# The spatial gating's layernorm, moved behind its transposes

## The reference

```
def _spatial_gating(u, v, ln_g, ln_b, w_s, b_s):
    u = jax.nn.gelu(u)
    v = _layernorm(jax.nn.gelu(v), ln_g, ln_b)          # mean and variance over the 256 channels
    vr = v.reshape(bn, ln // 128, 128, 4, ch // 4)
    mixed = jnp.einsum("gpq,bnqgc->bnpgc", w_s, vr) + b_s.T[None, None, :, :, None]
    return u * mixed.reshape(bn, ln, ch)
```

## Time and profile before

| what | value |
|---|---|
| median of three runs | 2793.08 us |
| the profiled execution's own time | 2795.46 us |
| its span, first to last instruction | 2793.7 us |
| TensorE busy | 2563.4 us, 92% of the span |
| VectorE busy | 1490.1 us, 53% |
| ScalarE busy | 727.0 us, 26% |
| GpSimd busy | 1051.5 us, 38% |

### The profile page before, as it was taken

How to read it: one execution, slowest core, us unless ns; L and a number is a source line. 1 busy time by engine, 2 the same in 40 slices (tenths; PEclk the granted TensorE clock), 3 DMA queues, 4 the chain that set the end, 5 groups by cost and what they waited for, 6 DMA issues and landing times.

```text
span 2793.7 us, 33113 instructions
## 1 busy us (share of the span) xinstructions
PE 2563.4 (92%) x12016; PEld 2054.9 (74%) x12016; DVE 1490.1 (53%) x2191; ACT 727.0 (26%) x1208; POOL 1051.5 (38%) x493
## 2 busy tenths in 40 slices
PE   8889999999989779999895999979889999999997
PEld 4768787777768767777674778868667777777775
DVE  5793036574711256544888544466764444444446
ACT  4311243434300045212312354433221000011012
POOL 2233333333346433447651111113554444333344
PEclk9999999999999889999997799989999999999998
DMA  7674453434366753233311222251211111111111
GB/s 281 227 290 173 131 159 128 142 124 136 125 222 204 292 205 143 74 129 125 130 46 51 63 80 77 67 182 42 68 61 46 46 46 45 47 51 45 45 45 68
DMA packets 131232, 325.24 MB, mean 116 GB/s; under 512 B 11568, under 2 KB 59248, under 8 KB 125616
## 3 DMA queue, kind: packets, MB, share of 16 engines
q1 hardware_dynamic: 93392, 223.50, 24.1%
q10 hardware_dynamic: 37728, 100.22, 9.9%
HBM read 248.57 MB, written 70.39 MB: 114 GB/s over the span
## 4 chain that ended last, share of the span: by engine, by line
PE 49%; DVE 8%; issue 3%; ACT 1%; DMA 0%; DVEq 0%; POOL 0%; SPq 0%; ACTq 0%
PE pb L478 36%; PE g L2981 6%; PE g L3054 2%; PE pb L2981 1%; PE g L3034 1%; DVE zcs L2246 1%; PE g L2962 1%; DVE f_spare L2455 1%; PE g L2835 1%; DVE xl L2158 0%; DMA kept_in<-cs_d 0%; PE g L2960 0%; DVE hl L2525 0%; DVE ml L2462 0%; DVE cb L2504 0%
## 5 line engine op out<-in xcount | busy, mean ns | idle before, releaser
L845 POOL TENSOR_TENSOR w_hi<-w_raw,one 128x1024 fp32r<-128x1024 f32 x191 | 399.7, 2093 | 1543.1 <-PE pb L478 1136.1
L478 PE MATMUL pb<-xh,w_hi 128*128 128x512 f32 (+1 forms) x1224 | 485.9, 397 | 46.2 <-POOL w_lo L848 17.0
L848 POOL TENSOR_TENSOR w_lo<-w_raw,w_hi 128x1024 fp32r<-128x1024 f32 x191 | 510.1, 2671 | 15.0
L478 PE MATMUL pb<-xh,w_lo 128*128 128x512 f32 (+1 forms) x1224 | 477.1, 390 | 0.0
L478 PE MATMUL pb<-xl,w_hi 128*128 128x512 f32 (+1 forms) x1224 | 476.5, 389 | 0.0
L478 PEld LDWEIGHTS pb<-xh,w_hi 128*128 128x128 f32 x1224 | 235.7, 193 | 103.2 <-POOL w_lo L866 16.3
L478 PE MATMUL pb<-mh,w_hi 128*128 128x512 f32 x704 | 283.5, 403 | 15.0 <-DVE ml L2462 7.3
L478 PE MATMUL pb<-mh,w_lo 128*128 128x512 f32 x704 | 281.4, 400 | 0.0
L478 PE MATMUL pb<-ml,w_hi 128*128 128x512 f32 x704 | 281.2, 399 | 0.0
L478 PEld LDWEIGHTS pb<-xl,w_hi 128*128 128x128 f32 x1224 | 234.8, 192 | 51.6
L478 PEld LDWEIGHTS pb<-xh,w_lo 128*128 128x128 f32 x1224 | 235.4, 192 | 50.2 <-issue 1.0
(11 more groups left out here) (408 smaller groups left out, 4614.0 us busy)
## 6 DMA issues: line engine op xcount, KB each, us to landing
w_raw<-in_wall SPq DMA_DIRECT2D x205, 512.0 KB, 3.5
mod_later<-in_modw SPq DMA_DIRECT2D x28, 1024.0 KB, 6.1
proj_d<-stage ACTq DMA_DIRECT2D x40, 512.0 KB, 2.7
at_bias<-in_bias SPq DMA_DIRECT2D x64, 192.0 KB, 2.7
mod_raw<-in_modt SPq DMA_DIRECT2D x8, 1024.0 KB, 10.7
svt<-vt_d ACTq DMA_DIRECT2D x12, 512.0 KB, 4.6
vc<-proj_d SPq DMA_DIRECT2D x10, 512.0 KB, 5.7
vt_d<-spare_h ACTq DMA_DIRECT2D x10, 512.0 KB, 3.8
```

The costliest lines, as they stand in the source:

```text
L478: mm = pe.matmul(pb[bank][:, 0:n], w[:, b, wc:wc + P], x[:, k, tokens], start=(count == 0), stop=(count == total - 1))
L845: nc.gpsimd.tensor_tensor(w_hi[:, b, :], w_raw[:, b, :], one[:, 0:1].to_broadcast([P, 1024]), ALU.mult).then_inc(w_high, 1)
L848: nc.gpsimd.tensor_tensor(w_lo[:, b, :], w_raw[:, b, :], w_hi[:, b, :], ALU.subtract).then_inc(w_split, 1)
```

## The change

The values are no longer normalised while channels lie on the partitions. The sixteen transposes come first, straight from `zcs[:, 6:8]`. With tokens on the partitions, mean and variance are sums along a row, one number per partition and chunk, kept in the new small tile `vstat`: ScalarE takes them with the accumulator output of eight copies (sum) and eight squares with the negative mean as bias (sum of squares), takes the square root of eight numbers per partition, VectorE inverts them, and ScalarE normalises in eight instructions. Both `gating_means` go. The channel scale and bias no longer act on `v`: the scale comes into the eviction of the gating products (line 2299 before), and the bias, times the row sums of `w_s`, is added to `sgb_sb` once, from four small matmuls into the fifth bank of `g`. SyncE's bias loads wait for ScalarE's squares in place of VectorE's multiplication.

```diff
--- before.py
+++ after.py
@@ -144,6 +144,7 @@
         both_gain = keep("both_gain", [P, KT])
         both_root = keep("both_root", [P, KT])
         dec = keep("dec", [P, NC, 8])
+        vstat = keep("vstat", [P, 4, NCX])
         ident, mean_d, mean_v, mean_g = (mat[:, n, :] for n in range(4))
         arena = place["next"]
 
@@ -368,8 +369,7 @@
         low_keys, z_at = at("zkr", [P, TA], arena + 107 * KB, F32R)
         zcs, a = at("zcs", [P, 8, T], z_at)
         hpad, a = at("hpad", [P, 2, T + TAPS - 1], a)
-        vsq, b = at("vsq", [P, 2, T], a)
-        vroot, _ = at("vroot", [P, T], a)
+        vsq, b = at("vsq", [P, NCX, C], a)
         vtok, c_ = at("vtok", [P, NCX, 256], b)
         sgw_sb, c_ = at("sgw_sb", [P, 4, P], c_)
         sgb_sb, _ = at("sgb_sb", [P, 2, P], c_)
@@ -787,8 +787,7 @@
                 bc, br, j = step_of(s)
                 sp.dma_start(at_bias[:, s % 4, :], bias6[br, bc, s // 16, j]).then_inc(bias_in[s % 4], 16)
 
-            sp.wait_ge(y_pe, 2)
-            sp.wait_ge(y_dve, 3)
+            sp.wait_ge(y_act, 2)
             for s in range(4):
                 bias_load(s)
             for s in range(STEPS):
@@ -1450,27 +1449,32 @@
                 return pb[u % 2]
 
             u_k, u_v, u_q, u_k1, _ = PAIR_UNITS
+            act.wait_ge(y_pe, 2)
+            for n in range(NCX):
+                v = act.activation(vtok[:, n, :], g[:, n // 2, C * (n % 2):C * (n % 2) + C], ACT.Copy,
+                                   accum_out=vstat[:, 0, n:n + 1])
+            v.then_inc(y_act, 1)
             pair_k_high(0, 0, pair_unit(u_k))
             act.wait_ge(y_dve, 1)
-            act.activation(vsq[:, :, :], zcs[:, 6:8, :], ACT.Square).then_inc(y_act, 1)
+            act.wait_ge(xl_ready, 6 * KT)
+            for n in range(NCX):
+                v = act.activation(vsq[:, n, :], vtok[:, n, :], ACT.Square, bias=vstat[:, 0, n:n + 1],
+                                   accum_out=vstat[:, 1, n:n + 1])
+            v.then_inc(y_act, 1)
+            act.wait_ge(y_act, 2)
+            act.activation(vstat[:, 1, :], vstat[:, 1, :], ACT.Sqrt, scale=1.0 / C,
+                           bias=epsc[:, 0:1]).then_inc(y_act, 1)
             for n in (1, 2):
                 pair_k_high(0, n, pair_unit(u_k + n))
-            act.wait_ge(y_pe, 2)
-            act.activation(vroot[:, :].rearrange("p (u n) -> p u n", u=2), g[:, 4:6, :], ACT.Sqrt,
-                           bias=epsc[:, 0:1]).then_inc(y_act, 1)
             pair_values(0, 0, pair_unit(u_v), bank_free[u_v % 2])
             keys_across(0)
             pair_values(0, 1, pair_unit(u_v + 1), bank_free[(u_v + 1) % 2])
             act.wait_ge(y_dve, 3)
-            for t in range(2):
-                n, m = COL["sg_g"] + t, COL["sg_b"] + t
-                v = act.activation(zcs[:, 6 + t, :], zcs[:, 6 + t, :], ACT.Identity,
-                                   scale=col[:, n:n + 1], bias=col[:, m:m + 1])
+            for n in range(NCX):
+                v = act.activation(vtok[:, n, :], vtok[:, n, :], ACT.Identity, scale=vstat[:, 1, n:n + 1],
+                                   bias=vstat[:, 2, n:n + 1])
             v.then_inc(y_act, 1)
             pair_values(0, 2, pair_unit(u_v + 2), bank_free[u_v % 2])
-            act.wait_ge(y_pe, 3)
-            act.activation(vtok[:, :, :].rearrange("p (a n) c -> p a (n c)", a=4), g[:, 0:4, :],
-                           ACT.Copy).then_inc(y_act, 1)
             for n in range(2):
                 pair_q_high(0, n, pair_unit(u_q + n))
             queries_across(0)
@@ -1478,7 +1482,7 @@
             act.activation(zcs[:, 2:4, :], zcs[:, 0:2, :], ACT.Square).then_inc(z_act, 1)
             for n in range(2):
                 if n == 0:
-                    act.wait_ge(y_pe, 4)
+                    act.wait_ge(y_pe, 3)
                 pair_k_high(1, n, pair_unit(u_k1 + n))
             act.wait_ge(y_dve, 5)
             act.dma_start(cs_d[0:2].rearrange("t p n -> p t n"), zcs[:, 6:8, :]).then_inc(kept_out, 16)
@@ -2253,21 +2257,21 @@
             for k in range(KT):
                 ctx_low(k)
             taps(5, 14)
+            nc.vector.tensor_scalar(vstat[:, 3, 0:2], col[:, COL["sg_b"]:COL["sg_b"] + 2], float(C), None, ALU.mult)
+            dve.wait_ge(y_act, 1)
+            nc.vector.tensor_scalar(vstat[:, 0, :], vstat[:, 0, :], -1.0 / C, None, ALU.mult).then_inc(y_dve, 1)
+            dve.wait_ge(y_dve, 1)
             dve.wait_ge(y_pe, 1)
             for t in range(2):
-                v = nc.vector.tensor_tensor(zcs[:, 6 + t, :].rearrange("p (u n) -> p u n", u=2),
-                                            zcs[:, 6 + t, :].rearrange("p (u n) -> p u n", u=2),
-                                            g[:, 4:6, :], ALU.subtract)
-            v.then_inc(y_dve, 1)
+                nc.vector.scalar_tensor_tensor(sgb_sb[:, t, :], g[:, 4, P * t:P * t + P], vstat[:, 3, t:t + 1],
+                                               sgb_sb[:, t, :], ALU.mult, ALU.add)
             for n, (first, last) in enumerate(((14, 17), (17, 18), (18, 20))):
                 pair_k_low(0, n, pb[(u_k + n) % 2], bank_free[(u_k + n) % 2])
                 taps(first, last)
-            dve.wait_ge(y_act, 2)
-            nc.vector.reciprocal(vroot[:, :], vroot[:, :]).then_inc(y_dve, 1)
+            dve.wait_ge(y_act, 3)
+            nc.vector.reciprocal(vstat[:, 1, :], vstat[:, 1, :]).then_inc(y_dve, 1)
             dve.wait_ge(y_dve, 2)
-            nc.vector.tensor_tensor(zcs[:, 6:8, :], zcs[:, 6:8, :],
-                                    vroot[:, :].unsqueeze(1).to_broadcast([P, 2, T]), ALU.mult)\
-              .then_inc(y_dve, 1)
+            nc.vector.tensor_tensor(vstat[:, 2, :], vstat[:, 0, :], vstat[:, 1, :], ALU.mult).then_inc(y_dve, 1)
             for n, (first, last) in enumerate(((20, 23), (23, 25))):
                 taps(first, last)
                 pair_q_low(0, n, pb[(u_q + n) % 2], bank_free[(u_q + n) % 2])
@@ -2293,13 +2297,13 @@
                                       [:, :, first:first + 32]).then_inc(at_sp, 1)
 
             at_stage(0)
-            dve.wait_ge(y_pe, 4)
-            dve.wait_ge(sg_in, 32)
+            dve.wait_ge(y_pe, 3)
             for t in range(2):
-                v = nc.vector.tensor_tensor(
+                n = COL["sg_g"] + t
+                v = nc.vector.scalar_tensor_tensor(
                     zcs[:, 6 + t, :].rearrange("p (n q) -> p n q", q=CH),
-                    g[:, 2 * t:2 * t + 2, :].rearrange("p a (n q) -> p (a n) q", q=CH),
-                    sgb_sb[:, t, :].unsqueeze(1).to_broadcast([P, NCX, CH]), ALU.add)
+                    g[:, 2 * t:2 * t + 2, :].rearrange("p a (n q) -> p (a n) q", q=CH), col[:, n:n + 1],
+                    sgb_sb[:, t, :].unsqueeze(1).to_broadcast([P, NCX, CH]), ALU.mult, ALU.add)
             v.then_inc(y_dve, 1)
             dve.wait_ge(y_dve, 4)
             nc.vector.tensor_tensor(zcs[:, 6:8, :], zcs[:, 6:8, :], zcs[:, 4:6, :], ALU.mult)\
@@ -2883,37 +2887,31 @@
                                        stop=True)
                 mm.then_inc(z_pe, 1)
 
-            def gating_means(src):
-                for n in range(2):
-                    for t in range(2):
-                        mm = pe.matmul(g[:, 4 + n, :], mean_v, src[:, t, H * n:H * n + H], start=(t == 0),
-                                       stop=(t == 1))
-                mm.then_inc(y_pe, 1)
-
             evicted(pe, UNIT[T_PAIR])
-            gating_means(zcs[:, 6:8, :])
-            pe.wait_ge(xl_ready, 6 * KT)
-            pe.wait_ge(xh_ready, 6 * KT)
-            pe_tile(pe, T_PAIR)
-            pe.wait_ge(y_act, 1)
-            pe.wait_ge(y_dve, 1)
-            gating_means(vsq[:, :, :])
-            pe_tile(pe, T_PAIR + 1)
-            pe.wait_ge(y_act, 3)
+            pe.wait_ge(sg_in, 32)
+            for q in range(4):
+                t, r = q // 2, 64 * (q % 2)
+                mm = pe.matmul(g[r:r + 64, 4, P * t:P * t + P], mean_v[:, 0:64], sgw_sb[:, q, :], start=True,
+                               stop=True)
+            mm.then_inc(y_pe, 1)
             for n in range(NCX):
                 for t in range(2):
                     o = (2 * n + t) * P
                     mm = pe.transpose(g[:, o // H, o % H:o % H + P], zcs[:, 6 + t, CH * n:CH * n + CH], ident)
             mm.then_inc(y_pe, 1)
+            pe.wait_ge(xl_ready, 6 * KT)
+            pe.wait_ge(xh_ready, 6 * KT)
+            pe_tile(pe, T_PAIR)
+            pe_tile(pe, T_PAIR + 1)
             pe_tile(pe, T_PAIR + 2)
             pe.wait_ge(z_cv, 2 * TAPS)
-            pe.wait_ge(y_act, 4)
+            pe.wait_ge(y_act, 1)
             conv_means(zcs[:, 0:2, :])
 
             def gating_products():
 
                 pe.wait_ge(z_dve, 1)
-                pe.wait_ge(sg_in, 32)
+                pe.wait_ge(y_act, 4)
                 for n in range(NCX):
                     for q in range(4):
                         t, r = q // 2, 64 * (q % 2)
```

## The result

The changed kernel has a median of 2766.83 us against 2793.56 us of the kernel before in the same comparison: a ratio of 0.9901 (95% interval 0.9888 to 0.9914), 26.7 us faster. Forecast were 9.4 us, with a range that ended at 2779.5. The direction held; the time lies outside.

The account below looks back on a forecast made before the run. VectorE's queue was taken as the bound: 9.6 us leave it, the port takes back 1.6, the lower clock 1.7, and a shorter wait for queries offsets part. Gain 9.4 us, from 2793.08 to 2783.7 us, range 2779.5 to 2788.5.

Parts of the forecast that it names:

- all behind them moves by 9.4: From the conv means on: again a gap of some 17 us and the lower clock, everything later shifted 9.4 us earlier.
- Points (a) to (g): New waits and moved work on VectorE, ScalarE, SyncE, TensorE and in the products' eviction: each hidden or worth nothing.
- What leaves VectorE's queue: VectorE ahead of the last tap: 11.05 us of instructions go, 1.45 come, so 9.6 us leave.
- second place: VectorE between taps (18, 20) and (20, 23): reciprocal and multiplication, 8.79 us, become two tiny instructions, 0.45 us.
- The port: VectorE and GpSimd hold each other up after the first small steps: 1.6 us net lost, ends -0.4 and 3.4.
- first place: VectorE between taps (5, 14) and the keys' low part: two subtractions, 2.3 us, become four small instructions, 1.0 us.
- rival 1: GpSimd gets in between two taps for both halves of its split: 1.8 us more, 2785.5 us; chance 17%.
- meeting at the queries: At taps (20, 23): one hold-up of VectorE by GpSimd's split, covered by VectorE's 3.3 us wait for first queries.
- The lower clock at the values: TensorE idles 5 us or more before the values, then runs at 0.50 for some 3 us, costing 1.7 us.
- what it was to hide: ScalarE's sums, squares, square root and normalising delay nothing; second keys' copies have 2 us or more to spare.
- rival 4: Before the second keys' copies ScalarE becomes the bound if a square exceeds 0.98 us; 2795.9 us at 2.5; chance 4%.
- rival 3: In the attention, 15 us longer at lower clock gives back 5.9 us: 2789.6 us, no tellable change; chance 8%.

Follow-up runs that it names:

- e2: The kernel before with an unused 128-byte tile where the changed kernel has `vstat`, nothing else: ratio 0.9963 to the kernel before, 10 us faster.
- e1: The changed kernel with `vstat` in a free place, so everything else in SBUF lies as in the kernel before: ratio 0.9939 to the kernel before.
- e9: The changed kernel measured once more, nothing altered, against the kernel before on one chip: ratio 0.9923, 21.5 us faster.
- e11: The kernel before with 128 unused bytes ahead of the inputs, more rounds on one chip: ratio 0.9957 to the kernel before, 12.0 us faster.
- e4: The kernel before with an unused 64-byte tile behind `dec`, ahead of the inputs: ratio 0.9888 to the kernel before, 31 us faster.

## Why the prediction was wrong

- **The step that failed** is none of the terms of the sum, but the premise ahead of them: that the parts outside the stretch have nothing of their own to gain and "all behind them moves by 9.4", with a unit of TensorE at 5.6 us as before. Points (a) to (g) cost the instructions of the change and never the one line that allocates `vstat`. That line moves the inputs of the big matrix products by 128 bytes against their weights: 4.2 ns less for each of some 7500 matmuls of 512 columns (e2 has it without the change, e1 the change without it). In the trace it is 13.7 us at the end and 3.2 at the front, of the 27.6 between the two profiled executions; the stretch itself gave 9.8, near the forecast. By the medians of e9 to e11 the shift alone is worth 12.0 us. The rest of the gap between traces goes with the granted clock, which differs from execution to execution; the sum had no term for it either.
- **What leaves VectorE's queue** was right. At the second place 8.79 us became 0.54 (0.45 forecast). From 1443.31 to the end of the last tap (1439.41 after) it was 9.0 us less, for 9.4. The two differ little partly because errors cancel: 8.25 us at the second place and 2.34 less waiting for `qa` came in, and 1.65 were lost to the port at taps (20, 23), which the forecast had left to that wait.
- **The port** was right in size and partly wrong in place. I charged 1.0 us for the small steps and 2.0 for the tap behind them. In fact the very first small instruction, on SBUF alone, stood 1.85 us until GpSimd's `w_hi` was done, and the pause took 2.49 us instead of 1.0; then the taps lost only some 0.2. Up to the second keys it is 11.35 us (1460.93 to 1472.28) for 11.76 forecast, and 11.36 before (1464.84 to 1476.20): the first place gave nothing. GpSimd's timeline after:

```profile
1449.14 13.62 POOL L844 TENSOR_TENSOR w_hi<-w_raw,one 128x1024 fp32r<-128x1024 f32 x1 [9.94 <-PE pb L478]
1462.84 2.35 POOL L847 TENSOR_TENSOR w_lo<-w_raw,w_hi 128x1024 fp32r<-128x1024 f32 x1
...
1490.88 2.15 POOL L844 TENSOR_TENSOR w_hi<-w_raw,one 128x1024 fp32r<-128x1024 f32 x1 [10.82 <-PE pb L478]
```

  The first row is again a wait through some ten taps (one instruction of 128x1024 each, as the prediction counts them) that the rule of the Trainium skill (SBUF — State Buffer, "SBUF: two separate sides") does not foresee; rival 1, which was that rule's (the prediction once calls it the second), did not come. This was no luck of one trace: `w_hi` at this place takes 12.26 to 12.56 us in all eight traces with the gating of before and 13.42 to 13.72 in all six with the changed one. Why it waits here and gets in after one instruction at other places is open. The last row is the meeting at the queries: taps (20, 23) took 8.91 us for 7.26, and VectorE's wait for `qa` shrank from 4.87 to 2.53, which covered it as said.
- **The lower clock at the values** came, but half of the wait was elsewhere. The forecast had TensorE idle for 5 us or more before the values; it waited 3.85 there, and 5.11 before the keys' third unit (3.3 before the change). Both waits were followed by a stretch at 0.50 (timeline, then windows):

```profile
1464.85 0.58 PE L478 MATMUL pb<-xh,w_hi 128*128 128x256 f32 x1 [5.11 <-DVE zkr L2221]
1473.82 0.77 PE L478 MATMUL pb<-xh,w_hi 128*128 128x512 f32 x1 [3.85 <-DVE zkr L2221]
```

```profile
1464.90:1468.00 3.10, 3.10 (x14) 3.10 (x15) 3.10 (x3) 3.08 (x10) 0.29 (x1) 0.50 0.54 149
1473.80:1477.00 3.20, 3.18 (x8) 2.52 (x9) 3.20 (x2) 0.00 (x0) 2.25 (x2) 0.50 0.02 5
```

- **ScalarE** hid what it was to hide. A square of 128x256 with its sum took 0.49 us from start to start, 0.98 being the limit of rival 4, and VectorE did not wait for the statistics:

```profile
1462.89 0.51 ACT L1461 ACTIVATE vsq<-vtok,vstat 128x256 f32<-128x256 f32 x1 [7.39 <-DVE vstat L2262]
...
1463.40 0.49 ACT L1461 ACTIVATE vsq<-vtok,vstat 128x256 f32<-128x256 f32 x1
```

- **The attention** (rival 3) moved as a block, 365.4 us for 366.3. But the traces of these kernels show it anywhere from 360.8 to 369.3 us, in step with its granted clock: 360.8 to 362.3 us at 0.94, 365.4 to 366.3 at 0.92, 367.4 to 369.3 at 0.91. So a forecast to the microsecond was never to be had from one trace.

## What to carry to other kernels

A new tile, however small, is an edit of every address behind it: before costing the instructions of a change, ask what it moves, and test that with an unused tile in its place. Where TensorE is the bound, look at the spacing of its matmuls over the whole trace, not only at the stretch that was edited. In this kernel a distance from weights to inputs that is a multiple of 512 bytes was worth more (31 us in e4) than the whole algebra of the gating (about 9.6).

## What the runs showed of the hardware

- The pace of a matmul of 128x512 (fp32r weights and inputs) depends on where its weights and its inputs lie to each other in SBUF: 227.2, 229.1, 232.9, 233.4 and 233.4 ns for distances of 0, 64, 128, 192 and 448 bytes modulo 512. What in the chip does this is not shown.
- The distance does not settle everything: the products of `ah` and `al` (383 pairs) kept 233.4 ns in the trace of the changed kernel, and have 229.0 in e9, the same kernel. That is open.
- A faster matmul need not bring a faster loop: the chunk loop went from 354.0 to 360.7 us with it, its granted clock from 0.98 to 0.95.
- A `TENSOR_SCALAR` of 128x2 on SBUF took 1.85 us beside GpSimd's running split, and one of 128x8 that came when the split was done 0.16.
